# Latent projections of a diffusion trunk by seven half-sized block products instead of eight, with sums on VectorE, and loads between the layers issued earlier

## What is computed

```
mod = silu(cond) @ ada_w + ada_b                  # six rows of 1024: shift, scale, gate, twice
xm  = rmsnorm(h) * (1 + sc1) + sh1                # (640, 1024)
proj = xm @ w_in                                  # columns: 768 qkv | 2064 other mixer inputs | 4096 gate logits
...
xm2 = rmsnorm(h) * (1 + sc2) + sh2
h   = h + g2 * hier_moe(xm2)                      # top expert group, top 2 experts in it, 16 experts
```

## Time and profile before

| | |
|---|---|
| median of 3 runs | 2391.94 us (2391.25 to 2393.18) |
| the profiled execution | 2391.63 us |
| its span in the trace | 2389.4 us |
| TensorE busy | 2224.2 us, 93% of the span |
| VectorE, ScalarE, GpSimd busy | 920.6, 561.4, 588.9 us |
| mean granted TensorE clock | 0.97 of full speed |

### The profile page before, as it was taken

The page is one execution under the profiler, slowest core; times in us unless marked ns, Lnnn a source line. Parts: engine busy times, 40 slices in busy tenths (PEclk is TensorE's granted clock), DMA queues, the critical chain, the costliest instruction groups (busy, mean ns, idle before and its releaser), DMA issues. The chain is left out here.

```text
span 2389.4 us, 32677 instructions
## 1 busy us (share of the span) xinstructions
PE 2224.2 (93%) x12912; PEld 1341.3 (56%) x12912; DVE 920.6 (39%) x1778; ACT 561.4 (23%) x1160; POOL 588.9 (25%) x588
## 2 busy tenths in 40 slices
PE   5999999999999998899969999999999999969993
PEld 2555667776676655333345556777767666533331
DVE  1000555545554435122230007555545543342224
ACT  3100231213444411111130002212234443111111
POOL 0000202325000620666210002033240026036651
PEclk9999999999999999899989999999999999979997
DMA  9332212113110953988573322111121148169854
GB/s 355 135 152 71 61 58 67 52 42 105 54 53 31 351 186 148 400 323 346 201 264 154 114 60 88 58 58 51 59 96 53 35 162 285 64 276 362 312 217 172
DMA packets 189415, 366.11 MB, mean 153 GB/s; under 512 B 54784, under 2 KB 130240, under 8 KB 175440
## 3 DMA queue, kind: packets, MB, share of 16 engines
q1 hardware_dynamic: 135568, 205.05, 24.9%
q0 software_dynamic: 39168, 134.29, 14.8%
q10 hardware_dynamic: 14528, 24.69, 3.0%
HBM read 431.46 MB, written 54.10 MB: 203 GB/s over the span
## 5 line engine op out<-in xcount | busy, mean ns | idle before, releaser
L593 PE MATMUL psum<-arena,h 128*128 128x320 f32 x2048 | 622.1, 446 | 11.4 <-ACT h L611 8.5
L593 PEld LDWEIGHTS psum<-arena,h 128*128 128x128 f32 x2048 | 370.9, 192 | 155.3 <-issue 15.9
L420 PE MATMUL psum<-arena 128*128 128x413 f32 (+3 forms) x1184 | 390.0, 490 | 6.4 <-ACT arena L447 6.4
L420 PEld LDWEIGHTS psum<-arena 128*128 128x128 f32 x1184 | 209.9, 192 | 177.7 <-issue 170.7
L1989 PE MATMUL psum<-arena 128*64 128x512 f32 x1152 | 262.6, 609 | 8.5 <-DMA arena<-in_moe_w,wrow 5.6
L1694 POOL DMA_INDIRECT arena<-in_moe_w,wrow x144 | 162.2, 1127 | 231.4 <-DVE wrow L2232 188.0
L1989 PEld LDWEIGHTS psum<-arena 128*64 128x64 f32 x1152 | 82.6, 140 | 163.5 <-issue 159.5
L474 DVE COPY arena<-psum 128x413 f32<-128x413 f32 (+2 forms) x36 | 17.6, 489 | 333.1 <-PE psum L420 333.1
L1855 PE MATMUL psum<-arena 128*128 128x320 f32 x512 | 138.9, 433 | 3.7 <-ACT arena L2034 1.9
L1866 PE MATMUL psum<-arena 128*128 128x512 f32 x320 | 141.2, 595 | 0.0
L2012 PE MATMUL psum<-arena 128*64 128x512 f32 x576 | 131.4, 598 | 0.9 <-ACT arena L2092 0.9
(11 more groups left out here) (338 smaller groups left out, 2776.5 us busy)
## 6 DMA issues: line engine op xcount, KB each, us to landing
arena<-in_ada_w SPq DMA_DIRECT2D x24, 2048.0 KB, 9.9
h<-in_w_in SPq DMA_DIRECT2D x32, 1024.0 KB, 5.5
gate_rows<-h SPq DMA_DIRECT2D x128, 160.0 KB, 1.8
arena<-gate_rows SPq DMA_DIRECT2D x16, 1280.0 KB, 11.2
y_rows<-arena ACTq DMA_DIRECT2D x72, 256.0 KB, 6.5
arena<-in_w_in SPq DMA_DIRECT2D x8, 1652.0 KB, 6.6
arena<-in_w_out SPq DMA_DIRECT2D x4, 2048.0 KB, 17.8
arena<-in_w_branch SPq DMA_DIRECT2D x12, 512.0 KB, 8.8
```

What stands on the lines that cost most here:

```text
L420: ins = nc.tensor.matmul(psum[:, 4 + i % 4, 0:w], lhs, rhs, start=(k == 0), stop=(k == KD - 1))
L593: ins = nc.tensor.matmul(psum[:, gate_bank(i), 0:HT], gw[c % 2][:, k, f:f + P], gate_xt[:, k, half:half + HT], start=(k == 0), stop=(k == ...
```

## The change

Chunk 0 stays as it was (414 columns now). In all other chunks the context tokens keep the plain product, and the 512 latent tokens are multiplied by Winograd's form of Strassen's scheme: tokens (256 + 256), inputs (512 + 512) and columns (two halves) are cut in two, and seven products of half-sized blocks replace eight. The qkv columns are now three chunks of 256, so there are eight chunks in all. VectorE makes four sums of activation blocks once per layer (`xs1` to `xs4`, two of them in the memory of `h[:, 0:2]`), four sums of weight blocks per chunk, and adds the products into the outputs; ScalarE copies the first product and the context items. The order of the two gate weight loads changes, because `gw[0]` now holds `xs2` and `xs3` until the last chunk.

Between the layers, two halves of `mod` and the weights and biases they need are loaded during the last visits of the experts (into `early_slots`) and computed ahead of the first transpose; chunk 0 has its own buffer and is loaded earlier; VectorE takes half of `copy_turned` for tile 0; and the last `store_y` of each layer is made in two halves. The gathers go to another place. Some semaphores are added.

```diff
+        TW = 414
-        chunks = tok_chunks[:1] + [(0, 512), (512, 256)] + tok_chunks[1:]
+        chunks = tok_chunks[:1] + [(0, 256), (256, 256), (512, 256)] + tok_chunks[1:]
+        units_in = [0] + [1 if f else 2 for f in is_feat[1:]]
+        PRODUCTS = 7
+        KH, HALF = KD // 2, LAT // 2
+        x11, x12, x21, x22 = xt[:, 0:KH, xa], xt[:, KH:, xa], xt[:, 0:KH, xb], xt[:, KH:, xb]
+        xs2, xs3 = (h[:, i, :].rearrange("p (k n) -> p k n", k=KH) for i in range(2))
+        xs1, xs4 = (ar(TMP + i * D, KH, HALF) for i in range(2))
...
+        first_chunk = ar(MODB + 768, KD, TW)
+        early_slots = [ada_slot(XT), ada_slot(PTOK)]
+        EARLY = lambda layer: 2 if layer else 0
...
         def load_later_chunks(sp, S, layer):
...
             for n in range(3, len(chunks)):
-                sp.wait_ge(S["proj_ps"], items_of(n - 3))
+                if n == 3:
+                    sp.wait_ge(S["proj_ps"], NT)
+                else:
+                    sp.wait_ge(S["pr_ps"], PRODUCTS * units_before[n - 2])
                 load_chunk(sp, S, layer, n)
-                m = n - 2
-                sp.wait_ge(S["mod_ps"], m)
-                load_ada_half(sp, layer, 2 + m // 2, m % 2, slotN, S["aw"])
-            sp.wait_ge(S["mod_ps"], 5)
-            load_ada_half(sp, layer, 4, 1, slotN, S["aw"])
+                m = n - 2 + e
+                if m < 6:
+                    sp.wait_ge(S["mod_ps"], m)
+                    load_ada_half(sp, layer, 2 + m // 2, m % 2, slotN, S["aw"])
             sp.wait_ge(S["xm"], NT)
             sp.wait_ge(S["h_out"], 16)
-            for c in range(2):
-                load_gate_weights(sp, S["gate_w"], c, layer)
+            load_gate_weights(sp, S["gate_w"], 1, layer)
             sp.wait_ge(S["row_done"], 3)
             store_ada(sp, layer, 2, 3, rowsN, S["stored_mod"])
+            sp.wait_ge(S["pr_ps"], product_at(len(chunks) - 1, 4, 0))
+            load_gate_weights(sp, S["gate_w"], 0, layer)
             sp.wait_ge(S["gate_w"], 32)
             sp.wait_ge(S["stored_mod"], 16 * 2)
...
+                def product(i, p, x, wt):
+                    g = product_at(n, i, p)
+                    if g >= 4:
+                        name, count = taken_by[g - 4]
+                        pe.wait_ge(S[name], count)
+                    for k in range(KH):
+                        lhs, rhs = (wt[:, k, :], x[:, k, :]) if feat else (x[:, k, p * P:(p + 1) * P], wt[:, k, :])
+                        ins = nc.tensor.matmul(product_out(n, i, p), lhs, rhs, start=(k == 0), stop=(k == KH - 1))
+                    ins.then_inc(S["pr_ps"], 1)
...
+                if not feat:
+                    context(0)
+                for p in units:
+                    product(0, p, x11, b11)
+                if feat:
+                    context(0)
+                for p in units:
+                    product(1, p, x12, b21)
+                pe.wait_ge(S["tsum"], n)
+                for p in units:
+                    product(2, p, xs2, t2)
+                for p in units:
+                    product(3, p, xs3, t3)
+                if feat:
+                    context(1)
+                for p in units:
+                    product(4, p, xs1, t1)
+                for p in units:
+                    product(5, p, xs4, b22)
+                for p in units:
+                    product(6, p, x22, t4)
...
+            if e:
+                pe.wait_ge(S["aw"], 16 * e)
+                for m in range(e):
+                    ada_half(m % 2, early_slots[m], 2).then_inc(S["mod_ps"], 1)
...
+        def copy_turned_half(v, own, S):
+            v.wait_ge(S["nt_ps"], 1)
+            for k in range(KD // 2, KD):
+                ins = nc.vector.tensor_scalar(xt[:, k, 0:P], bank(0, 2)[:, k * P:(k + 1) * P],
+                                              mcol[:, 2, k:k + 1], mcol[:, 0, k:k + 1], ALU.mult, ALU.add)
+                own.send(ins, S["own_v"] if k < KD - 1 else S["nt_v"])
...
+            v.wait_ge(S["nt_done"], NT)
+            v.wait_ge(S["h_out"], 16)
+            own.link(nc.vector.tensor_tensor(xs1, x21, x22, ALU.add))
+            own.link(nc.vector.tensor_tensor(xs2, xs1, x11, ALU.subtract))
+            own.link(nc.vector.tensor_tensor(xs3, x11, x21, ALU.subtract))
+            own.link(nc.vector.tensor_tensor(xs4, x12, xs2, ALU.subtract))
...
+                v.wait_ge(S[f"w{n % 3}"], 16 * (n // 3 + 1))
+                if n == 1:
+                    v.wait_ge(S["proj_ps"], NT)
+                else:
+                    v.wait_ge(S["pr_ps"], PRODUCTS * units_before[n])
+                own.link(nc.vector.tensor_tensor(t1, b12, b11, ALU.subtract))
+                own.link(nc.vector.tensor_tensor(t2, b22, t1, ALU.subtract))
+                own.link(nc.vector.tensor_tensor(t3, b22, b12, ALU.subtract))
+                own.tell(nc.vector.tensor_tensor(t4, b21, t2, ALU.subtract), S["tsum"])
...
+                for p in units:
+                    c11, c12, c21, c22 = blocks[p]
+                    combine(3, p, c21, c22)
+                for p in units:
+                    c11, c12, c21, c22 = blocks[p]
+                    combine(4, p, c12, c22, False)
+                    combine(4, p, c22, c21)
...
             def experts_sync(sp):
...
+                if not last:
+                    sp.wait_ge(X["h_ps"], MT - 2)
+                    load_ada_half(sp, l + 1, 2, 0, early_slots[0], X["aw"])
                 sp.wait_ge(X["h_ps"], MT - 1)
                 clear(sp, "merge")
...
-                    sp.wait_ge(X["y_ps"], MT - 1)
+                    load_ada_half(sp, l + 1, 2, 1, early_slots[1], X["aw"])
                     load_chunk(sp, X, l + 1, 0)
+                    load_ada_rows(sp, l + 1, 2, 3, biasN, None, None, X["rows_in"])
...
                 def store_y(j):
                     at = column_of(j)
+                    if j == MT - 1:
+                        v.wait_ge(stX[j % 2], 32 * (j // 2))
+                        v.wait_ge(X["y_half"], 1)
...
+                        v.wait_ge(X["y_ps"], j + 1)
```

More of the change, by code:

```diff
@@ L9 @@
+import itertools
 import math
@@ new lines, in weight_sums, with result_blocks @@
+        def weight_sums(n):
+            half = chunks[n][1] // 2
+            return [ar(MODB + 768 + i * KH * half, KH, half) for i in range(4)]
+        def result_blocks(n, p):
+            at, half = chunks[n][0], chunks[n][1] // 2
+            if is_feat[n]:
+                f, lo = at // P, 6 + CTX
+                return [qpre[:, f + c, lo + r * HALF:lo + (r + 1) * HALF] for r in range(2) for c in range(2)]
+            x0 = at - QKV_COLS
+            return [ptok[:, 1 + 2 * r + p, x0 + c * half:x0 + (c + 1) * half] for r in range(2) for c in range(2)]
@@ L439, in tile_std @@
+            for n in range(1, len(chunks)):
+                m = n - 1 + e
+                if m < 6:
+                    pe.wait_ge(S["aw"], 16 * (m + 1))
+                    ada_half(m % 2, slotN, m // 2).then_inc(S["mod_ps"], 1)
+                project_chunk(n)
         def tile_std(own, S, t, junk):
@@ L1709, in build @@
             yv = ar(XB + 4352, 2, D)
-            fin = [ar(PTOK + 4 * TOK_COLS + i * D, D) for i in range(10)]
+            fin = [ar(OALL + 4096 - (10 - i) * D, D) for i in range(10)]
             fjunk, fout, fgain = ar(PTOK, D), ar(PTOK + D, NT, D), ar(PTOK + 6 * D, D)
@@ L2340, in experts_vector @@
                     add_in(t)
+                    if t == 1 and not last:
+                        copy_turned_half(v, own, X)
                     if last and t >= 1:
```

209 lines of the change are left out of this document (138 added, 71 removed).

## The result

The changed kernel takes 2354.54 us (2351.91 to 2356.83, 4 runs) against 2392.29 (2391.25 to 2393.18) for the kernel before on the same chip: ratio 0.9843, 95% interval 0.983 to 0.9856. The time saved is 37.8 us; forecast were 30.0. The forecast time was 2361.9, with a range from 2354 to 2374; the measured one is just inside its lower end. The profiled execution took 2354.35 us, with 2.2 of it outside the span.

The account below looks back on a forecast made before the run. TensorE, busy 2224 of 2389 us, was taken as the bound. Terms -28.4, -3.8, -1.5, -1.1, +4.5 and +0.3 sum to -30.0, giving 2361.9 us, range 2354 to 2374.

Parts of the forecast that it names:

- The products: Projection stages, chunks after the first: seven half-sized products replace eight, saving 14.2 us a layer, -28.4 in all.
- the line can't be beaten: Bound on the projection products: time follows 0.83 ns a column, so at best 14.8 us a layer is saved.
- The rule cited in the prediction: TensorE products: weight loads overlap running matmuls only on different row groups, so loads would be paid in full; estimate 132 us.
- Halves of mod: Gap between the layers: two of layer 1's six halves move into TensorE's idle time, -3.8 us, zero if transfers land late.
- Copy and store between the layers: VectorE takes half of the first copy, -1.5 us; the last store goes in halves, -1.1 us over both layers.
- The end of the second stage: Second projection stage's end: gate load waits for products, constants for its landing, delaying the next block: +4.5 us (0 to +6.5).
- Semaphores: After the projection stages SyncE clears 6 and 8 more semaphores: +0.3 us.
- steps 1 and 2: Projection products, -28.4 us, and two halves of mod moved into the gap ahead of layer 1, -3.8 us.
- The stage's end costs nothing: Rival, second projection stage's end: the 4.5 us loss vanishes, giving 2357.4 us; chance 0.16.
- The loads come late: Rival, between the layers: delayed transfers for the early halves, edits there give nothing and 2 us are lost, 2369; chance 0.08.
- TensorE waits for VectorE: Rival, projection chunks: sums not hidden, 55 us in all, 2417; half of it 2389; chance 0.05.
- Weight loads come out: Rival, projection products: weight loads no longer hidden under shorter products, in full 137 us, 2499; chance 0.03.

Follow-up runs that it names:

- products_only: Changed kernel without the early loads and halves of mod between the layers, the split copy and the split store: 2357.98 us, 0.9858 of the kernel before.
- eight_products: Changed kernel with the seventh product of every half-sized unit computed twice, so eight again: 2383.11 us, 0.9967 of the kernel before.
- loads_only: Kernel before with only the edits between the layers and at the last store, whole products kept: 2383.63 us, 0.9968 of the kernel before.
- again: Changed kernel unaltered, run in a later session: 2351.25 us, 0.9831 of the kernel before.
- sums_x2: Changed kernel with VectorE making the four weight sums of each chunk twice: 2354.43 us, 0.9851 of the kernel before.
- sums_x3: Changed kernel with VectorE making the four weight sums of each chunk three times: 2376.46 us, 0.9939 of the kernel before.
- warm: Changed kernel with six useless halves of mod added on TensorE behind the two early ones between the layers: 2353.27 us, 0.9834 of the kernel before.
- before_again: Kernel before unaltered, run in a later session for a second trace: 2391.8 us, ratio 0.9999.
- warm7_consts_2: Changed kernel with constants issued ahead of the last gate weight load and seven useless halves of mod in the gap: 2348.91 us, 0.9822 of the kernel before.
- warm_consts: Changed kernel with six useless halves of mod in the gap and constants issued ahead of the last gate weight load: 2352.47 us, 0.9834 of the kernel before.
- consts_early: Changed kernel with constants issued ahead of the last gate weight load and its wait: 2349.34 us, 0.9822 of the kernel before; repeated, 2349.08 us, 0.982.

## Why: the prediction step by step

The mechanism was the one forecast: TensorE has fewer columns to move, pays nothing for the shorter ones, and waits for nobody. The sum was 7.8 us too small, and that the range held was in part luck: its lower end, 2354, was put 3 us below the case in which the end of the second stage costs nothing. That case didn't come; other stages made up for it. By its own steps:

**The products, -28.4 forecast, -30.6 measured.** Chunks 1 to 7 went from 175.2 to 159.9 us in the first layer (-15.3). In the second they went to 155.74, with two halves moved too; products_only, where they are not, has 159.88 there (-15.3). The step was mis-sized by 2.2. The interpolated distances, 1.39, 1.41 and 1.74, were 1.38, 1.40 and 1.73 or less; and the 0.6 a layer that I took off for borders and for the excess of short items was not there: 155.74 is under the 148.1 plus four halves at 1.93, 155.8, with no border at all. The bound "the line can't be beaten" was wrong by a little: -14.8 a layer was to be the most. The rule cited in the prediction (the Trainium skill, TensorE: Matmul & The Clock Gate, Part 3, The mechanism) doesn't hold here: all of these products use all row groups, and 204 columns come every 0.1725 us; were the load serial even at 0.111, it would be 0.28 or more. eight_products shows the same by the price of a further product.

**Halves of mod, -3.8; measured -4.1:** chunks 1 to 7 of the second layer take 155.74 us beside 159.88 in products_only, and loads_only has 171.1 for the 175.2 of before. Nothing is lost in the gap: they start at once, and the transposes wait for VectorE as before.

**Copy and store between the layers, -1.5 and half of -1.1; measured -1.4 and -0.9**, read at the starts above. Of the 0.9 the halved store gives 0.5, near the forecast, and a shorter transfer the rest. The 1.1 us which the first ten records took longer is no loss of the change: in fourteen traces they took 5.16 to 6.49, and 5.16 and 6.42 in two of the kernel before. The last store at the kernel's end gave 0.4.

**The end of the second stage, +4.5; measured +2.6.** The place, the cause and the order were right: load issued 8.2 us before the end, constants behind its landing, an idle time ended by them in the second layer only. Both landings were at the short end (4.95 and 6.3, not 5.5 and 6.5), and the 1.2 for a slower clock was not paid: the stretch table of the changed kernel holds the full clock through and behind the idle time.

```profile
1388.00:1390.00 2.00, 0.00 (x0) 0.00 (x0) 0.00 (x0) 0.00 (x0) 0.00 (x0) 1.00 0.74 314
...
1391.00:1396.00 5.00, 5.00 (x19) 3.57 (x20) 0.00 (x0) 2.88 (x3) 2.43 (x1) 1.00 0.10 1
```

The same place in the trace of products_only, behind an idle time of 3.53 us:

```profile
1395.00:1401.00 6.00, 5.63 (x15) 3.83 (x16) 0.00 (x0) 2.55 (x2) 2.88 (x1) 0.72 0.14 1
```

Six traces have 3.3 to 3.6 us of idleness there. The clock stayed full in after, again and sums_x2 and fell in products_only, sums_x3 and warm. Where it fell, the way from the first gate product to the next transposes took 74.26, 74.24 and 75.22 us, beside 74.22 to 74.38 where it didn't: the price was nothing twice and 0.9 once.

**Semaphores, +0.3.** In the first layer the next stage takes 0.1 to 0.4 us longer from its first gate product to its first transposes (74.99 to 75.16 with half-sized products, 74.79 and 74.93 in the kernel before, but 74.99 in loads_only too).

**What no step had.** The items measured make -15.0 to the first gate product (-15.3, with 0.2 for chunk 0 and 0.1 for the border), -1.0 between the layers (-2.2 to the first item, +1.1 behind it, rounded), -19.5 and +2.6 in the second stage, -0.4 at the end and +0.4 for semaphores: -32.9. The profiles differ by 37.3. The remaining 4.4 us lie in stages that the diff doesn't touch. I measured lengths from start to start in all fourteen traces, three with whole products (before, before_again, loads_only) and eleven with half-sized ones:

| stretch | whole products | half-sized products |
|---|---|---|
| first layer, DeltaNet after its first transposes | 262.69, 262.66, 262.80 | 259.86 to 262.85 |
| first layer, merge of the mixers | 70.60, 70.49, 70.47 | 69.03 to 69.81 |
| first layer, experts and gap | 248.00, 247.85, 244.99 | 245.15 to 248.55 |
| second layer, first gate product to DeltaNet's first transposes | 75.80, 74.10, 73.95 | 74.22 to 75.22 |
| second layer, DeltaNet after its first transposes | 260.75, 263.18, 261.03 | 258.96 to 259.39, and 262.15 |
| second layer, merge of the mixers | 69.68, 69.65, 69.57 | 69.16 to 69.42, and 70.44, 70.69 |
| attention of either layer | 186.7 | 186.7 |

Between before and after the two DeltaNet rows make -1.8 and -1.4, the fourth row -1.4, the merges -1.4 and -0.4. Against these stand +0.9 between the first merge and the experts and +0.8 in the experts themselves; the rest is small.

The differences in the DeltaNet rows and in the fourth are, in the main, the granted clock: TensorE ran part of the time at 1.2 in place of 2.4 GHz. In the first layer's DeltaNet before lost 3.4 us to it and after 1.7; that is nearly all of the -1.8 (what is left varies between 257.7 and 259.4 over the traces). In the fourth row before had one stretch at the lower clock that before_again and loads_only don't have. In the second layer's DeltaNet the clock is everything. The stretch table of that stage, each window with one stretch at the lower clock, for before, for after and for warm7_consts_2:

```profile
1512.00:1522.00 10.00, 10.00 (x65) 8.21 (x65) 4.09 (x15) 4.33 (x9) 0.00 (x0) 0.83 0.06 19
1529.00:1539.00 10.00, 10.00 (x48) 7.89 (x48) 4.70 (x10) 1.50 (x3) 0.00 (x0) 0.83 0.09 33
...
1493.00:1503.00 10.00, 10.00 (x45) 7.65 (x45) 4.13 (x9) 1.50 (x3) 0.00 (x0) 0.83 0.10 34
...
1471.00:1481.00 10.00, 10.00 (x65) 8.10 (x65) 4.85 (x16) 3.83 (x8) 0.00 (x0) 0.83 0.06 20
1488.00:1498.00 10.00, 10.00 (x44) 7.55 (x44) 3.92 (x9) 1.50 (x3) 0.00 (x0) 0.83 0.10 35
1703.00:1713.00 10.00, 8.51 (x35) 6.36 (x36) 3.02 (x6) 2.39 (x7) 9.21 (x11) 0.83 0.05 17
```

0.17 of 10 us is 1.7 us lost to the clock in each. In this DeltaNet stage before and loads_only lost 3.4 us, before_again 5.1, ten of the half-sized kernels 1.7 and warm7_consts_2 5.1; outside these stretches the clock was full. Without what the clock took, all fourteen traces have 257.0 to 258.1 us. So what sets the lengths in this row apart is time at the lower clock, and much of it came with half-sized products too, in warm7_consts_2. Ten of the eleven half-sized traces lost less to it than any of the three others; why was not settled.

The merge rows are one transfer. TensorE's second group of products waits for a sum, the sum for ScalarE, and ScalarE for the first load of `gate_rows`. The timeline at that place in before, in after, and in the second layer of warm:

```profile
780.31 0.83 ACT L2043 ACTIVATE arena<-arena 128x320 f32<-128x320 f32 x2 [3.39 <-DMA arena<-gate_rows]
781.35 4.84 PE L1855 MATMUL psum<-arena 128*128 128x320 f32 x17 [1.33 <-DVE arena L2133]
...
762.47 0.83 ACT L2214 ACTIVATE arena<-arena 128x320 f32<-128x320 f32 x2 [1.98 <-DMA arena<-gate_rows]
...
1918.18 0.83 ACT L2217 ACTIVATE arena<-arena 128x320 f32<-128x320 f32 x2 [3.23 <-DMA arena<-gate_rows]
```

The load lands between 3.2 and 4.9 us after the merge's first product, and in all 28 merges of the traces the merge takes 65.8 us more than that. In the first layer it lands at 4.6 to 4.8 with whole products and at 3.2 to 4.0 with half-sized ones, in the second it is late in warm and warm_consts, 4.6 and 4.9. What makes it late was not settled.

The row of the experts varies by 3.6 in both columns. So the 7.8 us that the sum lacked are 2.5 in steps 1 and 2, 1.9 at the stage's end and 4.4 in stages without an edit, less the 1.1 of the ten records. For the 4.4 the prediction had no term: they are stretches at the lower clock and one landing, less what the experts took longer. products_only was faster than its expectation by the same: its DeltaNet stages, its merges and the fourth row take 1.0, 1.4, 1.2, 0.3 and 1.5 less than in before.

**The rivals.** "The stage's end costs nothing" fell: it cost 2.6, and consts_early got 2.5 of it back in the trace, 1.9 in the time. Its forecast of 2357.4 is nevertheless nearer to the measured time than mine, for the reasons above. "The loads come late" fell on the timeline between the layers. "TensorE waits for VectorE" fell in the changed kernel and is what sums_x3 looks like. The cover of 2 us in a qkv chunk was too small: doubled sums, 2.9 us more, still fit. It is 3.6, mostly because a half of mod (1.93) stands ahead of every qkv chunk, and the prediction counted from behind it. "Weight loads come out" fell with the distance of 0.1725.

## What to carry to other kernels

Where TensorE is busy without a gap and VectorE idle, trading one product in eight for sums pays its full share of columns, as long as the sums are due later than they can be made; count that cover in the tightest chunk, since a wait costs its length and may cost clock too. A transfer that was free at an early place in a queue is not free once a wait is put ahead of it: look at what is queued behind every new wait. And a sum over the edited stages alone leaves out how untouched stages move: before a difference of 2 or 3 us is explained, the same stretch has to be seen in more than one trace of either kernel, and with the clock beside it.

## What the runs showed of the hardware

- The granted clock doesn't follow the length of one idle time. At the end of the second stage it stayed at 1.00 through 3.49 us of idleness in one trace and fell within 2 us after 3.53 us of it in another. It fell after 2.00 us in sums_x3, and in a wait of 1.65 us between the transposes and the first item in warm7_consts_2. In DeltaNet of the kernel before it fell between 1512 and 1522 us, where TensorE was busy for all of the 10 us. How long it stays down varies too: the same ten records took between 5.16 and 6.49 us. The Trainium skill (TensorE: Matmul & The Clock Gate, Part 1, What's actually happening) says that the number of matmuls run at the lower clock varies from run to run of one kernel; the traces agree, with 5.16 and 6.42 us in two of the kernel before.
- Adding 10 us of useless TensorE work to the gap between the layers left the transposes slow (1.97 us) and the time as it was. With 12 us, up to 1.67 before the transposes, these ran at the full clock (1.09), but the clock fell right behind them and no time was gained.
- Shorter records keep the line of columns: 0.1725 us for 204, 0.175 for 207, 0.216 for 256, beside 0.347 for 413 and 0.429 for 512 before.
- A stretch at the lower clock, with TensorE busy in it, cost 1.7 or 3.4 us, and a stage of 260 us lost between 1.7 and 5.1 us to such stretches in fourteen traces.
